# Attention of a hybrid transformer step: two heads pipelined apart in place of side by side

## What is computed

```python
def blocked_attention(q, k, v):
    ...
    def one_block(qblk):
        s = jnp.einsum('bqhgd,bkhd->bhgqk', qblk, k).astype(jnp.float32) * scale
        p = jax.nn.softmax(s, axis=-1).astype(v.dtype)
        return jnp.einsum('bhgqk,bkhd->bqhgd', p, v)
...
        mp = blocked_attention(qc, kc, vc) @ w_o[j]        # context: 128 queries, 128 keys
        k_all = jnp.concatenate([ks_, cache_k[:, j]], axis=1)
        v_all = jnp.concatenate([vs, cache_v[:, j]], axis=1)
        ms = blocked_attention(qs, k_all, v_all) @ w_o[j]  # latent: 512 queries, 640 keys
```

## Time and profile before

| | us |
|---|---|
| median of 3 runs (4215.59 to 4217.39) | 4217.21 |
| the profiled execution | 4209.3 |
| its span in the trace | 4207.5 |
| PE busy in the span | 4015.6 (95%) |
| DVE, ACT, POOL busy | 2789.8, 1751.2, 2321.4 |
| the attention stage, first scores to the output projection | about 178 |
| in it: PE, DVE, ACT busy | 137, 126, 117 |

### The profile page before, as it was taken

How to read it: one execution, slowest core, us unless ns; L and a number is a source line. 1 busy time by engine, 2 the same in 40 slices (tenths; PEclk the granted TensorE clock), 3 DMA queues, 4 the chain that set the end, 5 groups by cost and what they waited for, 6 DMA issues and landing times.

```text
span 4207.5 us, 57280 instructions
## 1 busy us (share of the span) xinstructions
PE 4015.6 (95%) x21230; PEld 3364.7 (80%) x21230; DVE 2789.8 (66%) x4311; ACT 1751.2 (42%) x3014; POOL 2321.4 (55%) x1112
## 2 busy tenths in 40 slices
PE   7978999999999899999989999999999989999997
PEld 5757898888888788877769989888888878887875
DVE  3773239889898566566643322989989867676665
ACT  3264324756657322322231132374655732222223
POOL 1101225676767666666643322576676767666664
PEclk9999999999999999999999999999999999999999
DMA  5303235867768988888844312486776898888884
GB/s 207 113 1 126 86 101 165 280 224 244 261 222 284 315 280 288 277 282 286 297 145 180 102 59 88 146 294 216 256 251 226 277 321 275 284 286 276 289 295 157
DMA packets 385364, 921.99 MB, mean 219 GB/s; under 512 B 29296, under 2 KB 161136, under 8 KB 370800
## 3 DMA queue, kind: packets, MB, share of 16 engines
q1 hardware_dynamic: 310432, 647.48, 46.0%
q0 software_dynamic: 73728, 268.47, 18.8%
q10 hardware_dynamic: 976, 3.15, 0.2%
HBM read 776.64 MB, written 142.34 MB: 218 GB/s over the span
## 4 chain that ended last, share of the span: by engine, by line
PE 32%; issue 30%; POOL 29%; DVE 4%; DMA 3%; ACT 1%; DVEq 0%; POOLq 0%; ACTq 0%
PE PS L736 21%; POOL SL L427 17%; POOL ROWS L434 9%; PE PS L544 5%; PE PS L728 4%; POOL SL L418 3%; DMA ROWS<-u_exp,EI 2%; PE PS L748 2%; DMA ROWS<-v_exp,EI 1%; PE PS L695 1%; DVE OH L1196 1%; DVE ROWS L1205 1%; DVE EQ L1177 0%; DVE EQ L1173 0%; ACT SH L963 0%
## 5 line engine op out<-in xcount | busy, mean ns | idle before, releaser
L427 POOL TENSOR_TENSOR SL<-RW,SH 128x1024 fp32r<-128x1024 f32 x512 | 1409.3, 2753 | 922.7 <-ACT SH L963 901.1
L963 ACT CAST SH<-RW 128x1024 fp32r<-128x1024 f32 x512 | 537.4, 1050 | 1063.8 <-PE PS L736 537.7
L736 PE MATMUL PS<-HH,SH 128*128 128x512 f32 x2048 | 815.9, 398 | 28.3 <-POOL SL L427 28.2
L748 PE MATMUL PS<-WH,SH 128*128 128x512 f32 x2048 | 811.2, 396 | 11.0 <-DVE WL L1255 5.6
L748 PE MATMUL PS<-WL,SH 128*128 128x512 f32 x2048 | 809.4, 395 | 0.0
L748 PE MATMUL PS<-WH,SL 128*128 128x512 f32 x2048 | 809.4, 395 | 0.0
L736 PE MATMUL PS<-HL,SH 128*128 128x512 f32 x2048 | 801.5, 391 | 0.0
L736 PE MATMUL PS<-HH,SL 128*128 128x512 f32 x2048 | 801.4, 391 | 0.0
L1211 DVE SCALAR_TENSOR_TENSOR ACC<-ROWS,AA,ACC 128x1024 f32<-128x1024 f32 x256 | 369.7, 1444 | 528.8 <-DMA ROWS<-v_exp,EI 522.3
L418 POOL TENSOR_TENSOR SL<-RW,SH 128x1024 fp32r<-128x1024 f32 x84 | 202.6, 2416 | 816.5 <-ACT SH L788 816.5
L1196 DVE TENSOR_TENSOR OH<-CO,PK 128x1024 f32<-128x1024 f32 x256 | 575.7, 2290 | 96.1 <-PE PS L728 88.0
(11 more groups left out here) (161 smaller groups left out, 5203.4 us busy)
## 6 DMA issues: line engine op xcount, KB each, us to landing
RW<-u_blk SPq DMA_DIRECT2D x256, 512.0 KB
RW<-v_blk SPq DMA_DIRECT2D x256, 512.0 KB
gate_acts<-GE SPq DMA_DIRECT2D x256, 256.0 KB
router_weights<-GT SPq DMA_DIRECT2D x64, 1024.0 KB, 5.2
GB<-router_weights SPq DMA_DIRECT2D x32, 2048.0 KB, 12.3
GL<-gate_acts SPq DMA_DIRECT2D x256, 256.0 KB
RW<-wstream SPq DMA_DIRECT2D x100, 512.0 KB
AW<-wpairs SPq DMA_DIRECT2D x40, 1024.0 KB, 5.1
```

The lines of the kernel that those rows point to most:

```text
L427: nc.gpsimd.tensor_tensor(SL[:, r % 2], RW[:, r % RAW], SH[:, r % 2].bitcast(F32), ALU.subtract).then_inc(raw_used, 1)
L736: last = mm(PS[:, n % 2], w[:, n % 2, j], a[:, j, 0:NS], start=(j == 0 and q == 0), stop=(j == DJ - 1 and q == 2))
L748: last = mm(PS[:, dj], w[:, k % 2, dj], a[:, k], start=start, stop=stop)
L963: nc.scalar.copy(SH[:, r % 2], RW[:, r % RAW]).then_inc(hi_done, 1)
```

## The change

The steps of a unit stay the same, in number and in shape; their order, their waits and one buffer are changed.

- PE: scores and values take a half as an argument. A step n is now, for half 0 and then for half 1: scores(n+1, half), values(n-2, half), turn(n, half). The two transposes of the cached keys are a part of their own after both halves, `turn_cached`, with a semaphore of its own (cached_turned, counted by `CACHED`). In scores and values the loop over halves is gone.
- scores(n, half) waits for the exponential of unit n-1 and the same half alone. The values are one unit further behind the scores than before.
- PT has two buffers by the parity of n, the second over the area WK.
- ACT: exponential of n half 0, copy of n-1 half 0, the same for half 1, the copy of the cached keys of n-1, out_high(n-2).
- DVE: normalisation of n half 0, maximum of n+1 half 0, the same for half 1, out_low(n-2).

```diff
-    PT, _ = sb("PT", [P, 2, NT], F32, at=at_H + 3 * NT * 4)
+    PT = [sb(f"PT{k}", [P, 2, NT], F32, at=at)[0] for k, at in enumerate((at_H + 3 * NT * 4, at_WK))]
...
-        def scores(n):
+        def scores(n, half):
             c, qt = UNITS[n]
             if n > 0:
-                pe.wait_ge(exp_done, 2 * n)
+                pe.wait_ge(exp_done, 2 * (n - 1) + half + 1)
...
+            a, b = half * HD, (half + 1) * HD
             for at, key in keys:
-                for half in range(2):
-                    a, b = half * HD, (half + 1) * HD
-                    o = half * 1024 + at
...
+                o = half * 1024 + at
+                last = mm(PSf[:, o:o + key.shape[-1]], BIG[a:b, c, qt * P:(qt + 1) * P], key[a:b],
+                          start=True, stop=True)
+            last.then_inc(score_done, 1)
 
         def turn(n, half):
             pe.wait_ge(p_done, 2 * n + half + 1)
             if n > 0:
-                pe.wait_ge(ptc_done, TURNED[n - 1])
-            for kt in range(key_tiles(n)):
+                pe.wait_ge(ptc_done, (TURNED[n - 2] if n > 1 else 0) + half + 1)
+            for kt in range(min(key_tiles(n), 4)):
...
-        def values(n):
+        def turn_cached(n):
+
+            if n > 0:
+                pe.wait_ge(ptc_done, TURNED[n - 1])
+            for half in range(2):
+                last = nc.tensor.transpose(PSf[:, 3072 + half * P:3072 + (half + 1) * P],
+                                           PR[n % 2][:, half, NS:NT], ID)
+            last.then_inc(cached_turned, 1)
+
+        def values(n, half):
             c, qt = UNITS[n]
             m, k = c // 4, key_tiles(n)
...
+            if half == 0:
+                pe.wait_ge(ptc_done, TURNED[n])
+                if n > 0:
+                    pe.wait_ge(oh_done, n)
             for kt in range(k):
-                for half in range(2):
...
         for n in range(len(UNITS)):
-            if n + 1 < len(UNITS):
-                scores(n + 1)
-            if n > 0:
-                values(n - 1)
-            turn(n, 0)
-            turn(n, 1)
-        values(len(UNITS) - 1)
+            for half in range(2):
+                if n + 1 < len(UNITS):
+                    scores(n + 1, half)
+                if n > 1:
+                    values(n - 2, half)
+                turn(n, half)
+            if key_tiles(n) > 4:
+                turn_cached(n)
+        for n in range(len(UNITS) - 2, len(UNITS)):
+            for half in range(2):
+                values(n, half)
...
         for n in range(len(UNITS)):
             for half in range(2):
...
-            if n > 1:
-                out_high(n - 2)
-            if n > 0:
-                turned(n - 1)
...
+                probabilities(n, half)
+                if n > 0:
+                    turned(n - 1, half)
+            if n > 0:
+                turned_cached(n - 1)
+            if n > 1:
+                out_high(n - 2)
...
         for n in range(len(UNITS)):
...
+                normalised(n, half)
+                if n + 1 < len(UNITS):
+                    largest(n + 1, half)
             if n > 1:
                 out_low(n - 2)
```

More of the change, by code:

```diff
@@ L225, in hybrid_step @@
                          "ptc_done", "pv_done", "o_done"))
-    oh_done = sem("oh_done")
+    oh_done, cached_turned = sem("oh_done"), sem("cached_turned")
     act_lo, conv_hi, conv_lo = sem("act_lo"), sem("conv_hi"), sem("conv_lo")
@@ L261, in key_tiles @@
         return 5 if UNITS[n][1] < 4 else 1
+    CACHED = [sum(int(key_tiles(b) > 1) for b in range(n + 1)) for n in range(len(UNITS))]
     TURNED = [sum(3 if key_tiles(b) > 1 else 2 for b in range(n + 1)) for n in range(len(UNITS))]
@@ L644, in turn @@
             if n > 0:
-                pe.wait_ge(ptc_done, TURNED[n - 1])
-            for kt in range(key_tiles(n)):
-                at = 2048 + half * 512 + kt * P if kt < 4 else 3072 + half * P
+                pe.wait_ge(ptc_done, (TURNED[n - 2] if n > 1 else 0) + half + 1)
+            for kt in range(min(key_tiles(n), 4)):
+                at = 2048 + half * 512 + kt * P
                 last = nc.tensor.transpose(PSf[:, at:at + P], PR[n % 2][:, half, kt * P:(kt + 1) * P], ID)
             last.then_inc(pt_done, 1)
-        def values(n):
+        def turn_cached(n):
[5 more added lines that the diff above has]
+            last.then_inc(cached_turned, 1)
@@ L652, in values @@
+        def values(n, half):
             c, qt = UNITS[n]
             m, k = c // 4, key_tiles(n)
-            pe.wait_ge(ptc_done, TURNED[n])
-            if n > 0:
-                pe.wait_ge(oh_done, n)
-            for kt in range(k):
-                for half in range(2):
[L659 to L667, removed]
@@ L668, in values @@
-            last.then_inc(pv_done, 1)
+            a, b = half * HD, (half + 1) * HD
+            if half == 0:
+                pe.wait_ge(ptc_done, TURNED[n])
+                if n > 0:
+                    pe.wait_ge(oh_done, n)
+            for kt in range(k):
+                if qt == 4:
+                    val = BIG[:, 10 + m, NS + a:NS + b]
+                elif kt < 4:
+                    val = BIG[:, 10 + m, kt * P + a:kt * P + b]
+                else:
+                    val = VC[:, m * P + a:m * P + b]
+                last = mm(PSf[a:b, 3584:3584 + P], val, PT[n % 2][:, half, kt * P:(kt + 1) * P],
+                          start=(kt == 0), stop=(kt == k - 1))
@@ L670, in _ @@
+            if half == 1:
+                last.then_inc(pv_done, 1)
         pe.wait_ge(vt_done, 2)
         pe.wait_ge(mod_done, 2)
-        scores(0)
+        scores(0, 0)
+        scores(0, 1)
         for n in range(len(UNITS)):
-            if n + 1 < len(UNITS):
-                scores(n + 1)
-            if n > 0:
-                values(n - 1)
-            turn(n, 0)
-            turn(n, 1)
-        values(len(UNITS) - 1)
+            for half in range(2):
[6 more added lines that the diff above has]
+                turn_cached(n)
@@ L908, in out_high, with probabilities @@
             nc.scalar.copy(HH[:, c, qt * P:(qt + 1) * P], PSf[:, 3584:3584 + P]).then_inc(o_done, 1)
-        def turned(n):
+        def probabilities(n, half):
             w = key_tiles(n) * P
[L912 to L917, removed]
+            act.wait_ge(nb_done, 2 * n + half + 1)
+            if n > 1:
+                act.wait_ge(pt_done, 2 * (n - 2) + half + 1)
+                act.wait_ge(cached_turned, CACHED[n - 2])
+            nc.scalar.activation(PR[n % 2][:, half, 0:w], PSf[:, half * 1024:half * 1024 + w], ACT.Exp,
+                                 bias=NB[:, half:half + 1], accum_out=RS[:, half:half + 1]).then_inc(exp_done, 1)
@@ new lines, in turned, with turned_cached @@
+        def turned(n, half):
+            w = min(key_tiles(n) * P, NS)
+            act.wait_ge(pt_done, 2 * n + half + 1)
+            nc.scalar.copy(PT[n % 2][:, half, 0:w],
+                           PSf[:, 2048 + half * 512:2048 + half * 512 + w]).then_inc(ptc_done, 1)
+        def turned_cached(n):
+            if key_tiles(n) > 4:
+                act.wait_ge(cached_turned, CACHED[n])
+                nc.scalar.copy(PT[n % 2][:, :, NS:NT], PSf[:, 3072:3072 + 2 * P].rearrange("p (h k) -> p h k", h=2)
@@ L928, in _ @@
+                if n > 0:
+                    turned(n - 1, half)
+            if n > 0:
+                turned_cached(n - 1)
             if n > 1:
                 out_high(n - 2)
-            if n > 0:
-                turned(n - 1)
-        out_high(len(UNITS) - 2)
-        turned(len(UNITS) - 1)
-        out_high(len(UNITS) - 1)
+        n = len(UNITS) - 1
+        turned(n, 0)
+        turned(n, 1)
+        turned_cached(n)
+        out_high(n - 1)
+        out_high(n)
         residual("wo", 1, "pq")
@@ L1334, in out_low, with largest, normalised @@
                             ALU.subtract).then_inc(oh_done, 1)
+        def largest(n, half):
+            w = key_tiles(n) * P
+            dve.wait_ge(score_done, 2 * n + half + 1)
+            v.reduce_max(MX[:, half:half + 1], PSf[:, half * 1024:half * 1024 + w], AX_X)
+            dve.drain()
+            v.tensor_scalar(NB[:, half:half + 1], MX[:, half:half + 1], -1.0, None, ALU.mult).then_inc(nb_done, 1)
+        def normalised(n, half):
+            dve.wait_ge(exp_done, 2 * n + half + 1)
+            v.reciprocal(RI[:, half:half + 1], RS[:, half:half + 1])
+            dve.drain()
+            pr = PR[n % 2][:, half, 0:key_tiles(n) * P]
+            v.tensor_scalar(pr, pr, RI[:, half:half + 1], None, ALU.mult).then_inc(p_done, 1)
+        largest(0, 0)
+        largest(0, 1)
         for n in range(len(UNITS)):
-            w = key_tiles(n) * P
             for half in range(2):
[L1339 to L1349, removed]
+                normalised(n, half)
+                if n + 1 < len(UNITS):
+                    largest(n + 1, half)
             if n > 1:
```

9 lines of the change are left out of this document (removed).

## The result

The changed kernel takes 4289.2 us (median of 4 runs, 4283.1 to 4293.2), the kernel before 4217.3 (4 runs, 4215.6 to 4221.6). The ratio is 1.0168, with a 95% interval of 1.015 to 1.0185: slower by 72 us, where 68 were forecast (4285). The profiled execution took 4293.2 us, its span is 4291.4.

The account below looks back on a forecast made before the run. It took a round of scores, maximum and exponentials to bound the kernel before, and PE the changed one. Groups +60.6, head +3 and tail +4.7 gave +68 us on 4217.2: 4285 us, range 4262 to 4303.

Parts of the forecast that it names:

- A pass alone costs what a pair costs: PE scores and values: heads apart cost double, so a large unit takes 6.47 us of PE, now 3.78.
- Rival 2: PE: weight loads of a lone half lie bare, +115 us more, 4400 us; chance 0.03.
- the rule weighed in the prediction: PE: a weight load runs beside a matmul in flight only when its row group differs, so lone halves would not hide loads.
- estimate of seven eighths of a pair: PE: a lone half priced from the skill table's 3.07 times speed for four row tiles; sum +48 us.
- the forecast's own sign of being wrong: PE profile after: two halves of different heads running at the same time in the new order would show the forecast wrong.
- The wait for the exponential behind the copy out: ScalarE queue: PE's scores wait for an exponential behind out_high(n-2), 0.39 or 0.9 us a time, 2.1 us a group.
- Rival 1: ScalarE queue: the exponential does not queue behind the copy as counted; 17 us less, 4268 us; chance 0.06.
- Rival 4: PE: each change of shape costs more than 0.2 us; +18 us, 4303; chance 0.05, shared with another further wait.
- The group: Five units mid-stage: PE's 27.9 us plus 2.1 of waits, 30.0 against 21.37; seven groups +60.6 us.
- The tail: Stage end, scores(39) to the last values: 11.7 us against 7.0, +4.7.
- The head: Stage start, scores(0) to scores(4): 23.0 us against 19.8, +3, with PE at 1.2 GHz for half of before's time.
- Rival 3: PE: a lone half costs half a pair; 4216 us unchanged or 4199 faster; chance 0.06, 0.03 each.

Follow-up runs that it names:

- Run 7: Kernel before with the maximum written negated by the reduction itself, so a drain and the multiplication by -1 go: 4201.1 us, ratio 0.9963.
- run 4: Changed kernel with ScalarE's copy out of unit n-2 moved behind the next unit's first exponential: 4278.0 us, ratio 1.0143 to the kernel before.
- Run 1: Kernel before with the loop over the heads made the outer one in scores and values: 4223.9 us, ratio 1.0020.
- run 5: Kernel before with values and turns of head 0, then values and turns of head 1; scores stay a pair: 4234.9 us, ratio 1.0046.
- run 10: Changed kernel as it is, measured again for comparison: 4286.0 us, ratio 1.0174 to the kernel before.
- runs 3: Changed kernel with the values a pair again, whole in the first half of a step, scores apart: 4238.9 us, ratio 1.0051 to the kernel before.
- run 2: Changed kernel with heads side by side again, keeping values two units behind and two PT buffers: 4217.1 us, ratio 1.0001 to the kernel before.
- run 9: Changed kernel with the scores of units 1 to 4 as a pair: 4281.9 us, ratio 1.0162 to the kernel before.

## Why the prediction was right, point by point

- **What bounds before:** the round of scores, maximum and exponentials. Run 7 took a drain and one instruction out of it and nothing else, and a large unit went from 4.37 to 3.95 us, the stage with it.
- **A pass alone costs what a pair costs:** right. Scores of one head take 1.27 us to the next shape (300.70 to 301.97; forecast 1.28), values 1.24 (301.97 to 303.21; 1.25), four transposes 0.59 (0.60). PE's bare work in a group is 27.72 us in run 4 (27.9). Rival 2, bare weight loads, is out, and so is the rule weighed in the prediction that would have led to it: the eight value passes on the same rows and columns take 1.09 us. So is the estimate of seven eighths of a pair: two lone passes of 512 take 1.12 us, two pairs 1.13.
- **The reason given for it was too simple.** The forecast took the order in the queue for the order on the array. Run 1 shows that heads apart in the queue still run side by side if nothing else stands between them and the other head is at most four passes off. In run 5 a single transpose between them, two places from pass to pass, ended it. In the middle of the changed kernel the other head is always five or more passes off, with transposes between, so either would do; no run tells which of the two keeps them apart there. At its ends the forecast's own sign of being wrong came true: passes of both heads at once, at 189.65 and 435.35.
- **The wait for the exponential behind the copy out:** 2.1 us a group forecast, 2.2 in the waits, 2.17 by run 4. Rival 1 falls with it. Rival 4 falls too: from the last pass of one shape to the first of the next it is 0.20 us with six changes a unit.
- **The group:** 30.04 forecast, 29.89 measured; seven groups grew by 59.2 us, where 60.6 were forecast.
- **The tail:** 11.7 forecast, 11.2 measured; the values of unit 38 ran in part side by side.
- **The head is the term that was mis-sized:** 23.0 forecast, 28.2 measured (31.05 in run 10). The step that failed is "PE has half of it at 1.2 GHz", taken from before. In before the granted clock was back at 2.4 GHz at 198.9 us; in the changed kernel at 214.3, in runs 3, 4 and 10 at 220 to 222. The low stretch in before, then in the changed kernel:

```profile
189.15:198.90 9.75, 6.75 (x25) 4.24 (x26) 4.92 (x11) 3.68 (x6) 0.00 (x0) 0.50 0.09 27
...
190.40:214.30 23.90, 21.92 (x61) 12.95 (x58) 10.58 (x26) 9.05 (x19) 0.00 (x0) 0.50 0.04 12
```

By its parts the head was forecast as 5.1, 7.1, 4.0 and 6.8 us and took 3.8, 7.4, 7.4 and 9.6 (from 189.65 to 193.46, 200.83, 208.21 and 217.85). The last two carry the late clock. The first was forecast with the heads one by one, and they ran side by side.
- **The sum:** the head's +5.2, with -1.4 on the groups and -0.5 on the tail, turns the forecast 68 into the 72 of the stage. That it missed by no more than 4 us is in part luck, since the smaller misses go against the large one.
- **The second PT buffer binds nobody:** right in the changed kernel. With pairs the depth gives 0.28 us a group (run 2), which the time of the kernel does not show.
- **Rival 3, the other side,** needed a lone half at half the price of a pair. The two tables by shape exclude it: the lone halves are busy for twice as long.

## What to carry to other kernels

Before two products on half arrays are pulled apart, count the engine's time with every pass alone: here that count, 27.9 us a group against a round of 21.4, gave most of the loss before anything ran (27.72 measured in run 4). What keeps such products together is that nothing else stands between them; the order of the loops matters less (+8 us in run 1, +17 with a few transposes between the values in run 5). And where a chain of engines sets the pace, first look for an instruction to drop from the chain: one negation gave -17 us (14 of them in the stage), where the new pipeline lost 72 and its depth alone gave nothing that could be measured.

## What the runs showed of the hardware

- TensorE starts a pass on the free half of the array ahead of passes that stand before it in the queue: the fifth beside the first, the eleventh beside the seventh (run 1), for row halves and for column halves. It did not do so over a single full-array transpose, whose weight load also waits for a semaphore (run 5).
- A change of shape costs about 0.16 us: ten transposes take 1.25 us up to the next shape's first pass, and ten times 0.109 is 1.09. From the last pass of one shape to the first of the next it is 0.20 us.
- The weight loads of lone passes on the same half are hidden: eight value passes take 1.09 us, as long as sixteen in pairs.
- The granted clock can stay at 1.2 GHz while PE is busy without a break. In run 10 PE was busy for all of the 10 us from 199 to 209 and the clock was at 0.50:

```profile
189.00:199.00 10.00, 7.09 (x18) 3.75 (x19) 4.76 (x11) 4.01 (x8) 0.00 (x0) 0.51 0.09 26
199.00:209.00 10.00, 10.00 (x28) 5.89 (x26) 4.25 (x11) 3.50 (x9) 0.00 (x0) 0.50 0.01 2
```

In the kernels with the scores side by side the clock was up at 199 to 200 us, in before after a stretch with PE busy for 6.75 of 9.75 us. That the late rise comes from single passes on half the array is suggested by run 9, not shown.
